# Head scaling and query tiles of the local attention shared with VectorE, and all eight masked bias additions ahead of the first maximum

## The reference, cut to what matters

```
q = rmsnorm(q.reshape(b, l, 8, 64), q_norm[i])
k = rmsnorm(k.reshape(b, l, 2, 64), k_norm[i])
scores = jnp.einsum('bnqhgd,bnkhd->bnhgqk', qb, kb).astype(jnp.float32) * (d ** -0.5)
scores = jnp.where(mask, scores, -jnp.inf)
m = jnp.maximum(scores.max(axis=-1, keepdims=True), sink)
p = jnp.exp(scores - m)
probs = p / (p.sum(axis=-1, keepdims=True) + jnp.exp(sink - m))
```

## Time and profile before

| | |
|---|---|
| median of 3 runs | 1336.87 us (1335.23 to 1338.18) |
| the profiled execution | 1336.47 us |
| its span in the profile | 1334.7 us |
| TensorE, VectorE, ScalarE, GpSimd busy | 1155.9, 657.3, 457.4, 42.9 us |
| the stage that the change touches | from 70.4 us to 96.4 us of the span |
| granted TensorE clock, mean | 0.943 of full |

### The profile page before, as it was taken

One profiled execution on the slowest core, in us unless ns is written; L12 is line 12 of the kernel. 1 busy time (PEld: TensorE's weight loads), 2 busy tenths in 40 slices (PEclk: granted clock), 3 DMA queues, 4 the chain that ended last, 5 costly groups with the idle time before them and its releaser, 6 DMA issues.

```text
span 1334.7 us, 20175 instructions
## 1 busy us (share of the span) xinstructions
PE 1155.9 (87%) x8324; PEld 910.0 (68%) x8324; DVE 657.3 (49%) x935; ACT 457.4 (34%) x575; POOL 42.9 (3%) x99
## 2 busy tenths in 40 slices
PE   7979999999999999999999999988557575656665
PEld 6868999999998999999998999863223131212211
DVE  7977555557788665556567687531011010101012
ACT  5565333335766433334364544331001010101001
POOL 5410000000000000000000000000000000000000
PEclk9999999999999999999999999989788787878879
DMA  8323555555434365556553546979999999999994
GB/s 241 145 99 127 183 196 189 187 180 168 158 127 159 128 210 188 177 179 215 175 172 107 193 160 238 413 310 422 421 422 422 422 422 422 422 422 422 422 421 205
DMA packets 139065, 343.43 MB, mean 257 GB/s; under 512 B 11890, under 2 KB 101124, under 8 KB 114420
## 3 DMA queue, kind: packets, MB, share of 16 engines
q1 hardware_dynamic: 137356, 338.09, 67.4%
q0 software_dynamic: 1536, 4.33, 1.1%
q10 hardware_dynamic: 104, 0.02, 0.0%
HBM read 341.36 MB, written 2.62 MB: 258 GB/s over the span
## 4 chain that ended last, share of the span: by engine, by line
PE 62%; DMA 23%; DVE 8%; ACT 3%; issue 2%; SPq 1%; POOL 0%; ACTq 0%; DVEq 0%; POOLq 0%
PE ps L1345 16%; PE ps L1347 15%; PE ps L1346 15%; DMA ring<-in_w_exp_down_dram 12%; DMA ring<-in_w_exp_up_dram 11%; PE ps L1887 4%; PE ps L1912 3%; SPq L539 1%; PE ps L1212 1%; ACT piece_hi L801 1%; DVE piece_lo L2087 1%; PE ps L1370 1%; PE ps L1363 1%; PE ps L1365 1%; PE ps L1485 1%
## 5 line engine op out<-in xcount | busy, mean ns | idle before, releaser
L2087 DVE TENSOR_TENSOR piece_lo<-ring,piece_hi 128x2048 fp32r<-128x2048 f32 x118 | 266.9, 2286 | 66.5 <-ACT piece_hi L801 65.9
L1345 PE MATMUL ps<-HT_hi,piece_hi 128*128 128x256 f32 x1008 | 286.6, 284 | 0.0
L1346 PE MATMUL ps<-HT_lo,piece_hi 128*128 128x256 f32 x1008 | 285.6, 283 | 0.0
L1347 PE MATMUL ps<-HT_hi,piece_lo 128*128 128x256 f32 x1008 | 285.6, 283 | 0.0
L801 ACT ACTIVATE piece_hi<-ring 128x2048 fp32r<-128x2048 f32 x118 | 222.9, 1912 | 172.7 <-PE ps L1347 146.5
L1887 PE MATMUL ps<-ring,arena 128*32 128x512 f32 x992 | 142.7, 728 | 86.8 <-DMA ring<-in_w_exp_up_dram 67.0
L1345 PEld LDWEIGHTS ps<-HT_hi,piece_hi 128*128 128x128 f32 x1008 | 193.8, 192 | 2.1 <-issue 1.2
L1346 PEld LDWEIGHTS ps<-HT_lo,piece_hi 128*128 128x128 f32 x1008 | 193.9, 192 | 0.9
L1347 PEld LDWEIGHTS ps<-HT_hi,piece_lo 128*128 128x128 f32 x1008 | 193.8, 192 | 0.0
L1887 PEld LDWEIGHTS ps<-ring,arena 128*32 128x32 f32 x992 | 39.0, 130 | 184.4 <-issue 183.9
L1912 PE MATMUL ps<-ring,arena 128*32 128x512 f32 x464 | 76.2, 765 | 52.2 <-DMA ring<-in_w_exp_down_dram 52.2
(11 more groups left out here) (460 smaller groups left out, 1776.2 us busy)
## 6 DMA issues: line engine op xcount, KB each, us to landing
ring<-in_w_exp_gate_dram SPq DMA_DIRECT2D x64, 1024.0 KB, 18.6
ring<-in_w_exp_up_dram SPq DMA_DIRECT2D x60, 1024.0 KB, 17.7
ring<-in_w_exp_down_dram SPq DMA_DIRECT2D x58, 1024.0 KB, 16.2
ring<-in_ffn_w_gate_dram SPq DMA_DIRECT2D x22, 1024.0 KB, 5.3
ring<-in_ffn_w_up_dram SPq DMA_DIRECT2D x22, 1024.0 KB, 5.4
ring<-in_ffn_w_down_dram SPq DMA_DIRECT2D x22, 1024.0 KB, 7.3
ring<-in_w_in_dram SPq DMA_DIRECT2D x20, 1024.0 KB, 5.3
ring<-in_odd_w_in_dram SPq DMA_DIRECT2D x12, 1024.0 KB, 5.3
```

What stands on the lines that cost most here:

```text
L1345: pe.matmul(out, sh, mh, start=start, stop=False, skip_group_check=True)
L1346: pe.matmul(out, sh, ml, start=False, stop=False, skip_group_check=True)
L1347: return pe.matmul(out, sl, mh, start=False, stop=stop, skip_group_check=True)
L2087: ve.tensor_tensor(piece_lo[k % RING][:, :], ring[:, k % RING, :], piece_hi[:, h % HI_SLABS, :].bitcast(F32), ALU.subtract).then_inc(split, 1)
```

## The change

Three edits, all in the stage above:

1. GpSimd scales only token block 0 and makes its two `kdup` copies. VectorE, directly behind `rsqrt` and its signal, scales block 1 and makes the other two copies, then raises `swa_r` to 2. TensorE waits for both ahead of turning the queries.
2. VectorE instead of ScalarE empties `swa_qT` 1, between `gelu(0)` and `gelu(1)`.
3. VectorE adds the masked bias of all eight heads first and then takes both sets of maxima.

```diff
-              ("q", ["a"]), ("ssm_k", ["a"]), ("q", ["a"]), ("swa_qT", ["a"] * 2), ("swa_kT", ["a"]),
+              ("q", ["a"]), ("ssm_k", ["a"]), ("q", ["a"]), ("swa_qT", ["a", "v"]), ("swa_kT", ["a"]),
...
             pool.wait_ge(swa_r, 1)
-            for tb in range(2):
-                r = sm[:, 140 + 10 * tb:150 + 10 * tb].unsqueeze(2).to_broadcast([P, 10, 64])
-                o.mark(pool.tensor_tensor(hd[:, tb], hd[:, tb], r, ALU.mult))
-            pool.wait_ge(g_order, o.count)
-            for tb in range(2):
-                for half in range(2):
-                    o.mark(pool.tensor_copy(kdup[:, tb, :, 64 * half:64 * half + 64],
-                                                  qkv[:, tb, 512:640].rearrange("p (k d) -> p k d", k=2)))
+            o.done(pool.tensor_tensor(hd[:, 0], hd[:, 0], sm[:, 140:150].unsqueeze(2).to_broadcast([P, 10, 64]), ALU.mult))
+            for half in range(2):
+                o.mark(pool.tensor_copy(kdup[:, 0, :, 64 * half:64 * half + 64],
+                                        qkv[:, 0, 512:640].rearrange("p (k d) -> p k d", k=2)))
...
-            for i in range(2):
-                empty("swa_qT", i, swa_qT[:, 2 * i:2 * i + 2, :], 2, scale=cols[:, ROW_QN:ROW_QN + 1])
+            empty("swa_qT", 0, swa_qT[:, 0:2, :], 2, scale=cols[:, ROW_QN:ROW_QN + 1])
...
             pe.wait_ge(swa_qn, 1)
+            pe.wait_ge(swa_r, 2)
...
             ve.nop().then_inc(swa_r, 1)
+            hd1 = qkv[:, 1, 0:640].rearrange("p (h d) -> p h d", d=64)
+            o.done(ve.tensor_tensor(hd1, hd1, sm[:, 150:160].unsqueeze(2).to_broadcast([P, 10, 64]), ALU.mult))
+            for half in range(2):
+                o.mark(ve.tensor_copy(kdup[:, 1, :, 64 * half:64 * half + 64],
+                                      qkv[:, 1, 512:640].rearrange("p (k d) -> p k d", k=2)))
+            ve.wait_ge(v_order, o.count)
+            ve.nop().then_inc(swa_r, 1)
...
             gelu(0)
+            empty("swa_qT", 1, swa_qT[:, 2:4, :], 2, scale=cols[:, ROW_QN:ROW_QN + 1])
             gelu(1)
-            masked_scores("swa", S0, local, range(4))
+            masked_scores("swa", S0, local, range(8))
             ve.wait_ge(misc_loaded, 16 * MISC_LOADS)
             local_maxima(0)
-            masked_scores("swa", S0, local, range(4, 8))
             local_maxima(1)
```

## The result

The changed kernel takes 1340.43 us at the median of 19 runs (1338.58 to 1342.01), the kernel before, run beside it, 1337.76 (19 runs, 1334.33 to 1339.4). The ratio is 1.0024, 95% interval 1.0017 to 1.003: slower by 3.2 us (2.3 to 4.0). The forecast, +3.1 us on 1336.87 with 1340.0 as the time and 1336.9 to 1342.4 as the range, holds.

The account below looks back on a forecast made before the run. TensorE's long run from 97 us was taken to bound the kernel, so its start decides. Terms 0.76 (first addition) + 1.1 (order) + 1.25 (clock) = +3.1 us on 1336.87 give 1340.0 us, range 1336.9 to 1342.4.

Parts of the forecast that it names:

- The start of the gelu: VectorE's first gelu argument: 2.5 us later, at 73.1, because VectorE's and GpSimd's simultaneous scalings block each other.
- Rival 1: Scaling and copies: no wait between VectorE and GpSimd, total +2.0 us, 1338.8 us, no difference; chance 0.17.
- The first addition: VectorE's first bias addition to the scores: starts at 78.77 instead of 78.01, +0.76 us.
- Eight additions first: First addition to end of ScalarE's exponentials: 13.59 us instead of 12.51, +1.1 us, both halves back to back.
- The `glu` matmuls: TensorE's hidden matmuls: end at about 88.5 instead of 91.96, gain nothing, and leave TensorE nearly idle afterwards.
- 1.71 us of work taken off GpSimd: GpSimd's scaling and copies at the stage's start: the saving buys nothing, queries being ready before ScalarE asks.
- The clock: TensorE's clock falls after idling, right ahead of its long run, where nothing hides it: +1.25 us, bounds 0 and 2.4.
- The nearest row: Earlier half-clock stretch, 84 to 87 us, losing 1.4 to 1.7 us hidden by glu; basis for the +1.25.
- Rival 3: TensorE's clock falls twice, also over the scores, delaying additions another 1.2 us: +4.3 us, 1341.2 us; chance 0.13.
- the long stretch: Low clock on TensorE's long run lasting half as long again: 2.4 us, the clock term's upper bound.
- The first two terms: Later first addition, +0.76 us, and later end of the exponentials from the eight-additions order, +1.1 us.
- a shift ahead of the long run goes through to the end: TensorE is busy 775.7 of 783 us from 97 to 880, so any shift of its start reaches the end.

Follow-up runs that it names:

- e5: Changed kernel with VectorE scaling both token blocks and making all four key copies, GpSimd only passing the signal on: 1340.75 us, ratio 1.0034 to the kernel before.
- e6: Kernel before with only the eight-additions-first order, plus 31 filling TensorE transposes in the late part: 1337.48 us, ratio 1.0005.
- e9: Kernel before with 14 filling TensorE transposes between the scores and the glu matmuls: 1337.97 us, ratio 1.0007.
- e3: Changed kernel with 31 filling TensorE transposes, put in late waits behind the scores: 1337.44 us, ratio 1.0007 to the kernel before.
- e1: Kernel before with only the third edit, all eight bias additions ahead of both sets of maxima: 1341.06 us, ratio 1.0025.
- e2: Changed kernel with additions and maxima back in two groups of four, so the sharing alone: 1338.48 us, ratio 1.0008 to the kernel before.
- e10: Kernel before with one edit, VectorE emptying turned probabilities 0 and 2 ahead of the gate products: 1334.86 us, ratio 0.9979.
- e4: Kernel before with the sharing, but VectorE's scaling and copies behind the first gelu argument, additions in the old order: 1335.3 us, ratio 0.9993.
- e7: Changed kernel with 31 late filling TensorE transposes and 16 more ahead of the scores: 1337.52 us, ratio 1.0002 to the kernel before.

## Why the prediction was right

**The start of the gelu: right.** `gelu_arg(0)` was predicted at 73.1 and starts at 73.37, of which 0.23 is upstream. The mechanism, one engine standing still for the other's whole instruction, is shown by e5. The scaling alone was taken at 0.82 us and is 0.78. The Trainium skill, SBUF — State Buffer, "Who interferes with whom", adds that the order of issue decides who blocks; the traces agree as far as they go: GpSimd, 0.01 us earlier by the record, ran its 1.26 us, and VectorE waited. Rival 1, a missed lock, didn't come in any of the profiles that have both scalings.

**The first addition: right.** 78.8 predicted, 78.93 found, 78.70 without the upstream part: +0.69 for the term +0.76.

**Eight additions first: right in mechanism and size.** ScalarE has no idle time between the halves. With the clock up the term is +1.03 (e6) for +1.1.

**The `glu` matmuls, taken at no gain: right** (e9), and so was their consequence, an idle TensorE behind them. They end at 89.77 instead of the 88.5 forecast, since the slow scores hold up their start; with the clock up they end at 87.84 (e6). (The prediction's 1.71 us of work taken off GpSimd is 1.74, half of the 3.47 in the earlier trace rows; nothing in the sum hangs on it.)

**The clock: the right mechanism, its size too small for the profiled execution.** The term was +1.25 with 2.4 as its upper bound; this execution paid 2.45, the trace of e3 gives 2.42 back, and the medians of e3 2.3, with over a microsecond of uncertainty and the clock near 725 us in it. The nearest row was a stretch of 84 to 87 us, some 3 us at half rate; the one that came lasts from about 93 to 103. I took off "what falls on transposes that wait anyway", but the last 12 don't wait for anything else: 1.29 of the 2.45 is theirs.

**Rival 3, a second fall over the scores, came in both profiles of the changed kernel**, and in those of e1, e2, e3, e5 and e10. It got 0.13. Its price was put at 1.2 us and was 0.84 (the additions take 4.66 us instead of 3.82), all of the 0.85 by which +1.88 exceeds the order's own 1.03. In other profiles it cost more, up to 1.9 us in e1. That e1 and e10 have it too, where nothing at that place has changed, says that it may come in executions of the kernel before as well.

So the two profiled executions of the changed kernel follow rival 3 with the long stretch, near the range's upper end (1341.87 and 1342.19 us), while the median, 1340.43, lies at the forecast. The parts of the first, by its trace and that of e6, are 0.69 for the start, 1.03 for the order, 0.85 for the early fall and 2.45 for the late one: 5.0 us, against 3.2 for the ratio of all runs.

**How much of it was luck.** The first two terms, 0.76 + 1.1, were right in mechanism and size. That the whole sum of +3.1 meets the measured +3.2 is partly luck: it leaves out the early fall and has half the price of the late one, and both profiled executions paid for both. What makes the median execution cheaper than these two is open: a fall may be missing or shorter in some executions of the changed kernel, or present in some of the kernel before. That a shift ahead of the long run goes through to the end is right up to the fall near 725 us, which came in some profiles and not in others, and adds or spares some 1.5 us.

## What to carry to other kernels

When two engines pass work to each other, the step that opens the other's work comes first, and added work goes into the wait behind it: one place down brought the first addition from 1.20 us later than before to 1.24 us earlier (e2, e4; 0.57 of the difference is e2's low clock), and grouping like instructions ahead of the first hand-over cost 1.03 us of overlap. Before giving half of an operation to an engine that would run it at the same moment as another, look in the trace for the two side by side: here one scaling in company takes longer than two alone. And of TensorE ask what it does in the microseconds ahead of a long run that starts on the critical path: finishing hidden work sooner there can cost more than it saves, as in the profile of e9. Last, follow a gain of a microsecond through to the end of the trace before you credit it to an edit: here some 1.5 us came or went 600 us behind the change.

## What the hardware showed that I had not expected

Removing a slow stretch that was hidden moved it onto the chain (e9, one profile): `glu` 1.7 us shorter, the run behind it 1.7 us longer. The low clock on TensorE ran from about 93 to 103 us, through matmuls that kept it busy from 97.75 on. And it is not settled by the program alone: with the same fillers behind the scores the late fall stayed away in e3 and e6 and came in e7, and the start of the stage, up to the scores the same program in before, e1, e6, e9 and e10, ran at half rate in e1 and e10 and at full rate in the other three. Near 720 us, far from any edit, the kernel before ran at 0.69 over 720 to 725 us around a wait of 1.89 us, and e3 at 1.00 around one of 1.87.
